# ScalarE evicts the first gate unit ahead of the value copies and the square roots

## The reference

```python
proj = xn @ cd_w_in[j]
lru_x, lru_g, m_x, m_o, m_if = split_cols(proj, CD_SIZES)      # 512, 512, 512, 512, 8
y_a = rglru_group(lru_x, lru_g, ...)
y_b = mlstm_group(m_x, m_o, m_if, ...)
...
# rglru_group: xc = causal convolution of lru_x, four taps
r_gate, i_gate = sigmoid(gates[0]), sigmoid(gates[1])          # gates = xc times small matrices
log_a = -LRU_C * r_gate * softplus(-lam)
u = sqrt(-expm1(2.0 * log_a)) * (i_gate * xc)
h = linear_recurrence(exp(log_a), u)
return h * gelu(gate)                                          # gate is lru_g
```

## Time and profile before

| | |
|---|---|
| median of 3 runs | 3100.81 us (3100.66 to 3103.07) |
| profiled execution | 3100.67 us, span 3098.9 us |
| TensorE (PE) busy | 2997.8 us, 97% |
| VectorE (DVE) busy | 1741.0 us, 56% |
| ScalarE (ACT) busy | 1272.6 us, 41% |
| GpSimd (POOL) busy | 318.4 us, 10% |

### The profile page before, as it was taken

How to read it: one execution, slowest core, us unless ns; L and a number is a source line. 1 busy time by engine, 2 the same in 40 slices (tenths; PEclk the granted TensorE clock), 3 DMA queues, 4 the chain that set the end, 5 groups by cost and what they waited for, 6 DMA issues and landing times.

```text
span 3098.9 us, 41482 instructions
## 1 busy us (share of the span) xinstructions
PE 2997.8 (97%) x17696; PEld 2469.0 (80%) x17696; DVE 1741.0 (56%) x2154; ACT 1272.6 (41%) x1702; POOL 318.4 (10%) x285
## 2 busy tenths in 40 slices
PE   8988889999999999999999998999999999999999
PEld 5877678778888766778888775689998888878998
DVE  6444454547544775546544745676666453566665
ACT  5443333434322564433322545544444333344443
POOL 1010000100000100000000200124310000013240
PEclk9999999999999999999999999999999999999999
DMA  5341023223332311323332331233332222233331
GB/s 186 113 112 29 29 72 127 96 68 96 95 91 90 111 61 55 109 68 95 95 88 92 92 90 28 55 96 99 105 110 92 85 86 98 69 89 102 100 107 67
DMA packets 340104, 274.89 MB, mean 89 GB/s; under 512 B 28768, under 2 KB 308832, under 8 KB 339408
## 3 DMA queue, kind: packets, MB, share of 16 engines
q1 hardware_dynamic: 335552, 252.83, 27.3%
q0 software_dynamic: 4368, 19.41, 1.9%
HBM read 263.83 MB, written 8.39 MB: 88 GB/s over the span
## 4 chain that ended last, share of the span: by engine, by line
PE 87%; DVE 6%; ACT 5%; issue 2%; POOL 0%; DMA 0%; DVEq 0%; SPq 0%; ACTq 0%; POOLq 0%
PE ps L189 86%; ACT arena L203 2%; ACT whi L206 1%; DVE arena L212 1%; DVE arena L220 1%; DVE wlo L212 1%; PE ps L192 1%; DVE hT L212 1%; DVE xlo L220 0%; ACT L203 0%; POOL arena L212 0%; DVE sml L229 0%; ACT arena L206 0%; DVE split L212 0%; DMA arena<-in_x 0%
## 5 line engine op out<-in xcount | busy, mean ns | idle before, releaser
L189 PE MATMUL ps<-split,whi 128*128 128x512 f32 (+1 forms) x3008 | 888.2, 373 | 14.6 <-DVE hT L212 6.0
L212 DVE TENSOR_TENSOR wlo<-wraw,whi 128x2048 fp32r<-128x2048 f32 (+5 forms) x261 | 565.8, 2170 | 485.1 <-ACT whi L206 484.5
L189 PE MATMUL ps<-xhi,whi 128*128 128x512 f32 (+2 forms) x2040 | 765.4, 380 | 17.4 <-DVE xlo L212 7.1
L189 PE MATMUL ps<-xhi,wlo 128*128 128x512 f32 (+2 forms) x1984 | 741.9, 374 | 0.0
L189 PE MATMUL ps<-xlo,whi 128*128 128x512 f32 (+2 forms) x1944 | 730.1, 376 | 0.0
L189 PEld LDWEIGHTS ps<-split,whi 128*128 128x128 f32 x3008 | 548.8, 189 | 131.2 <-issue 25.0
L206 ACT ACTIVATE whi<-wraw 128x2048 fp32r<-128x2048 f32 (+5 forms) x261 | 457.0, 1754 | 337.6 <-PE ps L189 237.2
L189 PE MATMUL ps<-split,wlo 128*128 128x512 f32 (+1 forms) x1504 | 553.6, 368 | 0.0
L189 PEld LDWEIGHTS ps<-xhi,whi 128*128 128x128 f32 (+1 forms) x2040 | 381.8, 189 | 101.1 <-issue 14.4
L189 PEld LDWEIGHTS ps<-xhi,wlo 128*128 128x128 f32 (+1 forms) x1984 | 374.5, 189 | 69.1 <-issue 5.1
L189 PEld LDWEIGHTS ps<-xlo,whi 128*128 128x128 f32 (+1 forms) x1944 | 365.8, 188 | 68.4
(11 more groups left out here) (132 smaller groups left out, 2430.6 us busy)
## 6 DMA issues: line engine op xcount, KB each, us to landing
wraw<-in_ffn_w_up SPq DMA_DIRECT2D x128, 512.0 KB, 5.2
wraw<-in_odd_w_in SPq DMA_DIRECT2D x24, 1024.0 KB, 5.1
wraw<-in_ffn_w_gate SPq DMA_DIRECT2D x44, 512.0 KB, 3.9
wraw<-in_ffn_w_down SPq DMA_DIRECT2D x20, 1024.0 KB, 5.2
wraw<-in_ffn_w_down SPq DMA_DIRECT2D x24, 768.0 KB, 4.4
wraw<-in_xattn_wkv SPq DMA_DIRECT2D x16, 1024.0 KB, 5.7
wraw<-in_xattn_wq SPq DMA_DIRECT2D x8, 1024.0 KB, 5.1
wraw<-in_xattn_wo SPq DMA_DIRECT2D x8, 1024.0 KB, 5.2
```

The lines of the kernel that those rows point to most:

```text
L189: return self.e.matmul(out, lhsT, rhs, start=start, stop=stop, skip_group_check=True)
L212: return self.e.tensor_tensor(out, a, b, op)
```

## The change

The two gelus of the first gate unit are issued within `convolved`, behind the third silu (`hd == 2`), and no longer by `project`, which keeps its turns. The second unit's gelus stay where they were.

```diff
@@ -2845,15 +2845,13 @@
-                    for name, _, _, blocks in u_g:
-                        W.round(act, name)
-                        yield
-                        for key, _, _ in blocks:
-                            act.wait_ge(S.P.of(*key))
-                            act.tables(ACT.Gelu_apprx_tanh)
-                            act.act(gel[:, key[1] * T:(key[1] + 1) * T], ps.ap(*key), ACT.Gelu_apprx_tanh).then_inc(
-                                *up(S.A, *key, frees=key))
-                        yield
+                    W.round(act, u_g[0][0])
+                    yield
+                    yield
+                    W.round(act, u_g[1][0])
+                    yield
+                    gated(1)
+                    yield
@@ -2914,12 +2912,21 @@
+                def gated(n):
+                    for key, _, _ in u_g[n][3]:
+                        act.wait_ge(S.P.of(*key))
+                        act.tables(ACT.Gelu_apprx_tanh)
+                        act.act(gel[:, key[1] * T:(key[1] + 1) * T], ps.ap(*key), ACT.Gelu_apprx_tanh).then_inc(
+                            *up(S.A, *key, frees=key))
+
                 def convolved():
                     yield from pause(9)
                     for hd in range(4):
                         act.wait_ge(S.V.of("mlstm_conv", hd))
                         act.tables(ACT.Silu)
                         act.act(xc_m[hd], xc_m[hd], ACT.Silu).then_inc(*up(S.A, "xc", hd))
+                        if hd == 2:
+                            gated(0)
                         if hd > 1:
                             yield
```

## The result

Over 20 executions each the changed kernel has a median of 3107.03 us (3098.34 to 3109.54) and the kernel before 3101.38 us (3096.48 to 3106.12). The ratio is 1.0015, 95% interval 1.0009 to 1.0021: slower, by 4.7 us (2.8 to 6.5). The profiled execution took 3104.83 us, its span is 3103.0 us. The forecast was 3103.7 us with a range of 3101.6 to 3105.8, so the median lies outside it, on the slow side. The direction was forecast, and so was a change of less than 0.2%.

A forecast was written before the change was run, and what follows sets the result against it. TensorE, busy 97% of the span, was taken to bound the kernel. Profiled 3100.67 us plus 0.93 for late scores and 1.99 for clock gave 3103.59; with 0.14 to the median, 3103.7 us, range 3101.6 to 3105.8.

The forecast's parts named there:

- The detour: On ScalarE, one table load and two gelus move ahead of the square roots, delaying them 2.40 us; ScalarE itself loses 0.
- Rival D: The inserted table load on ScalarE costs about 1.3 us more than its row, giving 3105.0 us; chance 5%.
- The gain on TensorE: Third gate block starts 2.4 us earlier; about 1.8 us of wait moves ahead of the maxima matmul; worth nothing.
- The price on the second chain: Late square roots pass through VectorE, silu and key copy, so head 0's score matmuls start 0.93 us late.
- The prediction's sign of being wrong: Score matmuls before 1128, third gelu ending before 1145, or a later wait in the layer shorter by two us or more.
- The clock: Score matmuls run at half clock behind the new wait of about 5 us, losing 1.99 us.
- The row near 227 us: Another TensorE wait, 4.60 us, with 5.20 us at half clock behind it, which would cost 2.6 us.
- Rival C: Clock costs more, through a longer fall and a second fall in this place: 3.6 us, giving 3105.3 us; chance 10%.
- The floor: The second chain reaches the output gate's first block 2.40 us late whatever TensorE does; TensorE's later arrival makes 2.92 us.
- Behind it: From the output gate TensorE is busy without a stop, so all that follows moves as one piece, no wait added.

The follow-up runs named there:

- e4: Kernel before, with VectorE copying gate blocks 0 and 1 out of PSUM and their gelus in place, ScalarE's order unchanged: ratio 1.0006 to the kernel before.
- profiles a and b: Second and third profiles of the unchanged changed kernel: output gate's block 0 starts 36.15 and 36.03 us after TensorE's matmuls behind gate block 1 start.
- e2: Changed kernel plus six unused TensorE matmuls ahead of head 0's scores, to keep the clock up: ratio 1.0004 to the kernel before.
- e3: Kernel before plus five unused TensorE matmuls in its wait for the first gelu, to keep the clock up: ratio 0.9999 to the kernel before.
- profiles b and c of before: Third and fourth profiles of the unchanged kernel before: output gate's block 0 starts 32.20 and 32.19 us after TensorE's matmuls behind gate block 1 start.
- e9: Kernel before plus one unused TensorE matmul ahead of the output gate's block 0, a pure delay: ratio 1.0000 to the kernel before.
- e10: Kernel before plus four unused TensorE matmuls ahead of the output gate's block 0, a pure delay: ratio 1.0013 to the kernel before.
- e7: Kernel before with VectorE copying gate blocks 0 and 1 out of PSUM and in-place gelus ahead of the square roots, behind the value copies: ratio 1.0016.

## Why the prediction was right or wrong

1. The detour: right. Load to load 1112.44 to 1115.82 with the two value copies in it; the first square root starts at +7.13 (1117.12 - 1109.99) in place of +4.72, 2.41 us later, and ScalarE reaches the load of the silu (1119.33) at +9.34, before at +9.32. No row here shows a drain beside a load: load, 0.02 us, next instruction. Rival D falls with it.
2. The gain on TensorE: right, and right that it is worth nothing in the end. The wait ahead of the maxima matmul is 1.81 us (about 1.8 said) and gate block 2 starts 2.47 us earlier (2.4 said). e4 shows that the whole 4.3 us would have been worth nothing either.
3. The price on the second chain: right. VectorE's wait for the root is 4.27 us (4.2 said), the scores start 0.85 us late (0.93 said), at the same place in all three profiles of the change within 0.02 us. The prediction's sign of being wrong, scores before 1128, has to be read with the 1.34 us: 1127.39 here is 1128.73 on the clock of the profile before, and the output gate's 1145.71 is 1147.05, just behind the 1145.9 to 1147 that was said.
4. The clock: the step that failed, in size. The prediction took 1.99 us from gate block 2 before the change. Between the scores and the output gate's block 0 lie 15.65 us before and 18.32, 18.74 and 18.61 in the three profiles of the change: 2.67, 3.09 and 2.96, mean **2.9 us**, about half of the 5.28, 6.14 and 5.88 us at half clock. The row near 227 us, which stood in the prediction as the other neighbour (2.6 us), was the nearer one, and the end I gave to this cost, 2.6 us, is below all three. What was wrong was to carry over the loss as it stood. Before the change the clock was at 0.50 from 1117.79 to 1124.61, 6.8 us, of which 2.50 us fell into the wait and cost nothing:

```profile
1117.79:1120.29 2.50, 0.00 (x1) 0.03 (x1) 2.36 (x3) 2.47 (x4) 0.00 (x0) 0.50 0.63 244
1120.29:1124.61 4.32, 4.32 (x10) 3.45 (x11) 4.04 (x7) 2.55 (x4) 0.00 (x0) 0.50 0.01 4
```

(The row of 3.98 us in the earlier trace rows ends before the clock rises.) In the three profiles of the change the clock was at 0.50 for 6.8 us as well, but only 1.55, 0.69 and 0.95 us of them lay in the wait. What decides how long after its start a wait meets the fall, no run here shows. Rival C, with its 3.6 us, had the mechanism of the excess, a longer stretch at half clock behind the wait; a second fall was there too in the profiles a and b (at 1118.7 and 1117.1, after the wait of 1.8 us), but it fell on gate block 2, which has some 5 us of cover, and cost nothing.
5. The floor: right. 2.40 us was said, e2 measures 2.41, and e3 shows the floor of 32.2 in the kernel before. So do the profiles b and c of before, where the scores start 0.4 and 0.3 us earlier and D is the same. It explains as well why the old wait's loss of clock was free and the new one is not.
6. Behind it: right within the layer. From the output gate to the layer's last stretch 76.30 us before and 76.33 after. Behind the layer it did not hold: "all that follows is moved as one piece" took the 1879.05 us of one profile for fixed, and there are 1880.98 to 1881.48 us in the three profiles of the change and 1878.98 to 1881.47 in the four of before.

The corrected sum is 0.85 + 2.91 = 3.76 us, which lies inside the ratio's interval (2.8 to 6.5 us). With it the forecast would have been 3104.5 us, still inside the range. So the larger part of the miss is elsewhere: in the range, which was built around one execution of 3100.67 us with 0.2 us for the spread. That was far too small: one of the three timings shown was 3103.07 us already. The median of before itself is 3101.38 over 20 executions and 3103.5 over those beside e9 and e10, the part behind the layer alone differs by 2.5 us between profiles of before, and the point from which D counts lies anywhere from 1109.76 to 1111.79.

3101.38 + 3.76 would be 3105.1; the remaining 1.9 us to the median of 3107.03 is open as to its cause. The list of executions shows where it stands, for the times lie in groups some 2 us apart. Before: 2 near 3096.5, 10 at 3100.3 to 3101.7, 6 at 3103.0 to 3103.7 and 2 at 3105.3 to 3106.1. The change: 1 at 3098.3, 5 at 3104.1 to 3104.9, 10 at 3106.8 to 3107.3 and 4 at 3108.8 to 3109.5. From group to group the last three are 3.4 to 3.8 us later, which is about what the layer costs; the rest is that the median of before lies in its cheaper group of these and that of the change in the next. Whether the change makes the dearer groups more frequent is not shown. All three profiles of the change had the dearer part behind the layer, and two of four of before, which is too few to say.

## What to carry to other kernels

A wait of the bottleneck engine is worth only what its next wait leaves. Before an eviction is put ahead, look at what it is put ahead of (here the square roots), follow that to the next point where the bottleneck engine waits, and compare the slacks there. 4.3 us gained at one wait came to nothing, because the key copy allowed the scores to start only 1.55 us earlier and the third gelu held the output gate where it was, 0.14 us behind. Idle time that moves takes its loss of clock with it, and where the old loss had cover the new one may have none. To price it, take the whole time at half clock of a like wait, from fall to rise, and not only the part that was left behind that wait: half of 6.8 us, 3.4 us, would have held as an upper end here, where 2.7 to 3.1 were measured. And take a spread from several executions, not from one profile.

## What the runs showed of the hardware

The time at half clock behind a wait does not grow with the wait. Behind waits for the key copy of 3.57, 3.61, 4.62, 5.13 and 7.1 us it was 6.14, 5.88, 4.96, 5.28 and 5.97 us (profiles a and b of the change, e4, the change, e7); with the part inside the wait, the clock was at 0.50 for 6.8 us in the first four and for 10.2 us in e7. Behind the wait of 1.8 us in this place the clock stayed at 1.00 in the first profile of the change and fell in a and b, on a stretch with cover. Six fp32 matmuls of 128x512 without use kept the clock at 1.00 through a wait of 5 us. And a fall need not stand behind the longest idle time: in the third profile of before TensorE idled for 2.4 us at 1899.5 and kept full clock, then for 1.3 us at 1906.0, and fell to half at 1907.9. The first profile of before has falls near 1903 and 1934 us, the third near 1908, 1932 and 1959, in the same code with the same waits, and 2.2 us lie between them in the part behind the layer. One profile of a kernel shows one such course.
